# One fused model block on one Trainium2 core: wide bias reads, one load of x, one turn for two norms, last combine over eight banks, two value groups 512 columns wide

## The reference, cut to what matters

```python
# block 1, x is [512, 1024] f32
z = rms_norm(x, norm_mix) @ w_in                       # u | q k v of 8 heads of 64
y_pool = multiscale_pool(u, ...)
y_attn = neighbourhood_attention(q, k, v, rpb)         # 8x64 grid, window 8 rows x 16 columns, bias from rpb
x = x + concat(y_pool, y_attn) @ w_out
x = x + expert_choice_ffn(rms_norm(x), ...)            # 16 experts, 64 tokens each, 25 MB of weights each
x = x + sigmoid(rms_norm(x, norm_ple) @ w_ple_gate) * rms_norm(p @ w_ple_proj)
# block 2
x = gmlp_layer(x, c, ...)
shift, scale = ada_mod(c, kv_ada_w, ...)
k, v = split((rms_norm(x, kv_g) * (1 + scale) + shift) @ w_kv)     # 3 groups x 2 heads of 128, each
shift, scale, gate = ada_mod(c, b_ada_w, ...)
q, z = split((rms_norm(x, b_g) * (1 + scale) + shift) @ w_in_b)    # the same x: 3 groups x 8 heads of 128
o = three dilated attentions (dilations 1, 4, 16), merged by their log sums
x = x + gate * ((o * silu(z)) @ w_out_b)
```

## Time and profile before

| | |
|---|---|
| time, median of 3 runs | 2253.64 us (2252.07 to 2254.20) |
| profiled execution, its own time | 2254.82 us |
| its span, first to last instruction | 2252.8 us |
| TensorE busy | 2063.3 us (92%) |
| VectorE, ScalarE, GpSimd busy | 926.1, 565.2, 47.8 us |
| mean granted clock of TensorE | 0.949 |
| experts' weights | 3 x 128 slabs of 1 MB |

### The profile page before, as it was taken

One profiled execution on the slowest core, in us unless ns is written; L12 is line 12 of the kernel. 1 busy time (PEld: TensorE's weight loads), 2 busy tenths in 40 slices (PEclk: granted clock), 3 DMA queues, 4 the chain that ended last, 5 costly groups with the idle time before them and its releaser, 6 DMA issues.

```text
span 2252.8 us, 24571 instructions
## 1 busy us (share of the span) xinstructions
PE 2063.3 (92%) x9309; PEld 1235.3 (55%) x9309; DVE 926.1 (41%) x1483; ACT 565.2 (25%) x974; POOL 47.8 (2%) x53
## 2 busy tenths in 40 slices
PE   5999989999999999999999789999999998989798
PEld 4766763332222222222222277888887786867687
DVE  2776451111111111111111255465455727696963
ACT  3332341111011010111110244432232323553510
POOL 3050000000000000000000000000000000000000
PEclk9975799999999999999999898999999999989899
DMA  9641239999999999999999834454242212011010
GB/s 182 224 135 57 82 145 393 422 422 422 422 422 422 422 422 422 422 422 422 422 422 422 332 112 150 172 184 138 94 171 75 75 40 90 21 57 56 20 38 38
DMA packets 134346, 529.81 MB, mean 235 GB/s; under 512 B 10374, under 2 KB 58308, under 8 KB 85124
## 3 DMA queue, kind: packets, MB, share of 16 engines
q1 hardware_dynamic: 131988, 523.69, 59.5%
q0 software_dynamic: 1712, 3.06, 1.1%
q10 hardware_dynamic: 576, 2.10, 0.4%
HBM read 526.56 MB, written 2.23 MB: 235 GB/s over the span
## 4 chain that ended last, share of the span: by engine, by line
PE 54%; DMA 33%; DVE 7%; SPq 2%; ACT 2%; issue 1%; ACTq 0%; DVEq 0%
DMA w_expert<-in_w_up 15%; DMA w_expert<-in_w_gate 15%; PE bank L757 6%; PE bank L758 6%; PE bank L759 6%; PE bank L947 6%; PE bank L777 5%; PE bank L779 5%; PE bank L778 5%; DMA raw<-in_w_in 2%; PE bank L834 2%; PE bank L789 1%; PE bank L848 1%; PE bank L957 1%; SPq L616 1%
## 5 line engine op out<-in xcount | busy, mean ns | idle before, releaser
L947 PE MATMUL bank<-w_expert,chosen 128*64 128x512 f32 x2048 | 483.7, 602 | 62.4 <-DMA w_expert<-in_w_up 46.2
L947 PEld LDWEIGHTS bank<-w_expert,chosen 128*64 128x64 f32 x2048 | 130.4, 136 | 395.7 <-issue 232.6
L757 PE MATMUL bank<-act_hi,w_hi 128*128 128x512 f32 x656 | 271.0, 413 | 18.6 <-DVE w_lo L1423 14.7
L1423 DVE TENSOR_TENSOR w_lo<-raw,w_hi 128x2048 fp32r<-128x2048 f32 x75 | 171.9, 2292 | 219.8 <-ACT w_hi L1149 219.8
L758 PE MATMUL bank<-act_lo,w_hi 128*128 128x512 f32 x656 | 257.1, 392 | 0.0
L759 PE MATMUL bank<-act_hi,w_lo 128*128 128x512 f32 x656 | 256.9, 392 | 0.0
L1661 DVE TENSOR_TENSOR x_res<-x_res,bank 128x512 f32<-128x512 f32 x136 | 87.4, 684 | 412.2 <-PE bank L966 412.2
L957 PE MATMUL bank<-w_expert,hidden_t 128*64 128x512 f32 x1024 | 229.9, 596 | 6.0 <-ACT hidden_t L1295 4.6
L1149 ACT CAST w_hi<-raw 128x2048 fp32r<-128x2048 f32 x75 | 142.6, 1901 | 199.9 <-PE bank L779 165.7
L1683 DVE TENSOR_TENSOR hidden_rows<-gate_silu,bank 128x512 f32<-128x512 f32 x32 | 20.6, 684 | 364.4 <-PE bank L947 364.4
L757 PEld LDWEIGHTS bank<-act_hi,w_hi 128*128 128x128 f32 x656 | 124.0, 189 | 56.4 <-DVE w_lo L1423 16.5
(11 more groups left out here) (239 smaller groups left out, 2465.4 us busy)
## 6 DMA issues: line engine op xcount, KB each, us to landing
w_expert<-in_w_gate SPq DMA_DIRECT2D x128, 1024.0 KB, 24.9
w_expert<-in_w_up SPq DMA_DIRECT2D x128, 1024.0 KB, 26.5
w_expert<-in_w_down SPq DMA_DIRECT2D x128, 1024.0 KB, 26.2
raw<-in_a_w_in SPq DMA_DIRECT2D x24, 1024.0 KB, 5.7
raw<-in_b_w_in SPq DMA_DIRECT2D x16, 1024.0 KB, 5.3
raw<-in_a_ada_w SPq DMA_DIRECT2D x12, 1024.0 KB, 5.1
raw<-in_b_ada_w SPq DMA_DIRECT2D x12, 1024.0 KB, 6.0
raw<-in_w_in SPq DMA_DIRECT2D x8, 1024.0 KB, 10.7
```

Source lines behind the costliest of these rows:

```text
L757: mm(b[:, :], hi[:, cols], ah[:, kc, :], start=(kc == 0), stop=False)
L947: last = mm(PS[b0 + n][HALF[x], :], XE[:, k % 4, HALF[k // 4]], WE[place][:, r], start=(k == 0), stop=(k == KD - 1), skip_group_check=True)
L1423: tt(WLO[w % 2][:, :], RAW[slot(n_of["W"][w])][:, :], WHI[w % 2][:, :].bitcast(F32), ALU.subtract).then_inc(lo_ready, 1)
```

## The change

1. **Bias.** `rpb_wide` is flat with 16 floats behind it. `BIAS` holds 63 floats per row in place of 48 and is read by two DMAs of 64 partitions, each partition in one piece of 4032 floats (16,128 bytes). They wait until ScalarE has copied chunk 3 of the first projection. `V1` moves from 176.5 to 112 KB to make room.
2. **x.** ScalarE's queue loads x once, in plain order, and behind it slab 0. The transposes of `norm(0)` write to the bank in grid order (`grid_tile`, a stride of eight elements). SyncE's second load of x is gone; `c_wins` and the bias row of the gate are loaded behind slab 7 in place of slab 1. The transpose of the parameter rows stands between the first six chunks and the last two, so that the eighth chunk's bank is that of chunk 0.
3. **Last combine.** Eight matmul results go to eight banks with no wait in between. VectorE adds them first and norms behind them, with the lower part of the first gate slab before the last norm tile and that of the second behind `norm_lo`. ScalarE casts the first gate slab, does the statistics and `norm_hi`, then casts the second.
4. **One turn.** For keys and values `norm(4)` goes into `BH`, `BL`; ScalarE copies each bank to `XT` as well. The queries' norm is scaled from `XT` into `AH`, `AL`, four chunks ahead of the copies of the values of groups 1 and 2 and four behind them. TensorE has no `norm(5)`.
5. **Values.** Group 0 goes by two chunks of `fm_chunk` into `VF` (in the place of `GATE_A`) and is turned by eight transposes. Groups 1 and 2, whose token order is the same, share one unit: 128 tokens stationary (stride four), 512 columns moving, over two slabs.

```diff
-    rpb_wide = nc.dram_tensor("rpb_wide", (ROWS, H1 * ROWS, 63), F32, kind="Internal").ap()
+    rpb_wide = nc.dram_tensor("rpb_wide", (ROWS * H1 * ROWS * 63 + 16,), F32, kind="Internal").ap()
...
-        V1 = at("v1", 176.5, [P, NT, 512])
-        BIAS = at("bias_master", 184.5, [P, H1 * ROWS, 48])
...
+
+        BIAS = at("bias_master", 176.5, [P, H1 * ROWS, 63])
...
-        W_VK = [slab("W", fm_src(a["w_kv_2"], 768 + 256 * g)) for g in range(NG)]
+        W_V0 = slab("W", fm_src(a["w_kv_2"], 768))
+        W_V12 = tm_slabs(a["w_kv_2"], 0, 1, 1024)[0]
...
+            if k == 5:
+                count["lo"] += KD
+                return
...
+                if k == 0 and kc == 6:
+                    note(("cols",), "dve")
...
+        def grid_tile(b, t):
+
+            return b[:, :].rearrange("p (c r) -> p r c", r=ROWS)[:, 2 * t:2 * t + 2, :]
...
-            for n in range(N_E - 1):
+            for n in range(1, N_E - 1):
                 load(n)
-                if n == 3:
-                    sp.wait_ge(n_xn, NT)
-                    for t in range(NT):
-                        sp.dma_start(X[:, t, :], a["x"][0, t * P:(t + 1) * P, :]).then_inc(s_x, 16)
-                if n == 1:
+                if n == 7:
                     sp.dma_start(CW[:, :], c_wins).then_inc(s_wins, 16)
...
-            pool.wait_ge(s_rpb, 16 * (ROWS + 1))
-            for c in range(16):
-                pool.dma_start(BIAS[c * ROWS:(c + 1) * ROWS, :, :],
-                               bass.AP(rpb_wide.tensor, c, [[H1 * ROWS * 63, ROWS], [63, H1 * ROWS], [1, 48]])
+            pool.dma_start(rpb_wide[ROWS * H1 * ROWS * 63:].rearrange("(a b) -> a b", a=1), RPB[0:1, 0, 0:16]).then_inc(s_rpb, 16)
+            pool.wait_ge(s_rpb, 16 * (ROWS + 2))
+            pool.wait_ge(freed["act"], fills[("in", 3)][2])
+            for half in range(2):
+                pool.dma_start(BIAS[half * 64:(half + 1) * 64, :, :].rearrange("p k j -> p (k j)"),
+                               bass.AP(rpb_wide.tensor, 8 * half, [[1, 8], [H1 * ROWS * 63, ROWS], [1, H1 * ROWS * 63]])
                                ).then_inc(s_bias, 16)
...
             pool.dma_start(WP[:, :, :], a["w_pool"][0].rearrange("g c d -> c g d")).then_inc(s_wp, 16)
-            pool.wait_ge(freed["act"], fills[("in", 3)][2])
...
+                        pe.wait_ge(d_add, ADDS - 2 if chunks[0] == 0 else ADDS)
                     for t in range(NT):
...
-                            last = nc.tensor.transpose(banks[kc][:, t * P:(t + 1) * P],
+                            last = nc.tensor.transpose(grid_tile(banks[kc], t) if k == 0 else banks[kc][:, t * P:(t + 1) * P],
...
+                    if k == 0 and chunks[0] == 0:
+                        pe.wait_ge(s_rows, 16 * (len(COL_ROWS) + 2))
+                        b = begin(("cols",))
+                        nc.tensor.transpose(b[:, 0:NCOL], ROWS_IN[0:NCOL, :], ident[0:NCOL, 0:NCOL]).then_inc(filled, 1)
...
+            pe.wait_ge(v_xe, NE + 1)
             for t in range(NT):
-                combine(t, 8 * NE)
-            pe.wait_ge(v_xe, NE + 1)
+                for x in range(2):
+                    mm(PS[2 * t + x][:, :], SELT[HALF[x], t * P:(t + 1) * P], Y[HALF[x], :], start=True, stop=True
+                       ).then_inc(m_c, 1)
...
-                fm_chunk(W_K[j // 2], j % 2, ("k2", j), AH, AL, 50 if j == 0 else None)
+                fm_chunk(W_K[j // 2], j % 2, ("k2", j), BH, BL, 50 if j == 0 else None)
...
-            for g in range(NG):
-                hi, lo = slab_ready(W_VK[g])
+            for c in range(KV2):
+                fm_chunk(W_V0, c, ("vf", c), BH, BL)
+            banks = []
+            for s in range(2):
+                hi, lo = slab_ready(W_V12[s])
                 for t in range(NT):
-                    b = begin(("v2", g, t))
-                    for kc in range(KD):
-                        a_hi, a_lo = tile_of(AH[:, kc, :], g, t), tile_of(AL[:, kc, :], g, t)
-                        r = slice(kc * 256, (kc + 1) * 256)
-                        mm(b[:, 0:256], a_hi, hi[:, r], start=(kc == 0), stop=False)
-                        mm(b[:, 0:256], a_hi, lo[:, r], start=False, stop=False)
-                        last = mm(b[:, 0:256], a_lo, hi[:, r], start=False, stop=(kc == KD - 1))
-                    last.then_inc(filled, 1)
-            norm(5)
+                    if s == 0:
+                        banks.append(begin(("v12", t)))
+                    for k in range(4):
+                        kc = 4 * s + k
+                        a_hi, a_lo = tile_of(BH[:, kc, :], 1, t), tile_of(BL[:, kc, :], 1, t)
+                        r = slice(k * 512, (k + 1) * 512)
+                        mm(banks[t][:, :], a_hi, hi[:, r], start=(kc == 0), stop=False)
+                        mm(banks[t][:, :], a_hi, lo[:, r], start=False, stop=False)
+                        last = mm(banks[t][:, :], a_lo, hi[:, r], start=False, stop=(kc == KD - 1))
+                    if s == 1:
+                        last.then_inc(filled, 1)
+                if s == 0:
+                    last.then_inc(half_used, 1)
+            pe.wait_ge(freed["act"], fills[("vf", 1)][2])
+            for t in range(NT):
+                b = begin(("v0", t))
+                for c in range(KV2):
+                    last = nc.tensor.transpose(b[:, c * P:(c + 1) * P], VF[:, c, t * P:(t + 1) * P], ident)
+                last.then_inc(filled, 1)
...
             for t in range(NT):
-                grid = bass.AP(a["x"].tensor, a["x"].offset + t * P // ROWS * D, [[D, P // ROWS], [S // ROWS * D, ROWS], [1, D]])
-                act.dma_start(X[:, t, :], grid).then_inc(s_xg[t], 16)
+                act.dma_start(X[:, t, :], a["x"][0, t * P:(t + 1) * P, :]).then_inc(s_x[t], 16)
+            act.dma_start(raw3(0, KD), stream[0][0]).then_inc(loaded[0], 16)
             split_at, f = [0], [0]
...
 
+            split_upto(W_PGATE[0][0])
+            stats(2, lambda t: (d_add, 8 * NE + 2 * t + 2))
+            norm_hi(2)
             split_upto(W_PGATE[0][1])
-            stats(2, lambda t: (d_add, 8 * NE + 2 * t + 2))
             act.wait_ge(k_step, 25)
             nc.scalar.activation(ERSTD, ESS, ACT.Sqrt).then_inc(k_exp, 1)
-            norm_hi(2)
...
-            norm_full(4)
+            for kc in range(KD):
+                b = take(("norm", 4, kc))
+                scaled(b[:, :], NORM_MUL[4](kc), NORM_ADD[4](kc), kv_full)
+                nc.scalar.copy(XT[:, kc, :], b[:, :]).then_inc(freed["act"], 1)
...
-                for t in range(NT):
-                    nc.scalar.copy(V2[:, g, t, :], take(("v2", g, t))[:, 0:256]).then_inc(freed["act"], 1)
+            split_upto(W_V0 + 1)
+            for c in range(KV2):
+                nc.scalar.copy(VF[:, c, :], take(("vf", c))[:, :]).then_inc(freed["act"], 1)
+            split_upto(W_V12[1])
             act.wait_ge(freed["dve"], fills[("k2", 5)][2])
-            norm_full(5)
+            for kc in range(4):
+                scaled(XT[:, kc, :], NORM_MUL[5](kc), NORM_ADD[5](kc), b_full)
+            split_upto(W_V12[1] + 1)
+            for t in range(NT):
+                nc.scalar.copy(V2[:, 1:3, t, :], take(("v12", t))[:, :].rearrange("p (g d) -> p g d", g=2)
+                               ).then_inc(freed["act"], 1)
+            for kc in range(4, KD):
+                scaled(XT[:, kc, :], NORM_MUL[5](kc), NORM_ADD[5](kc), b_full)
+            for t in range(NT):
+                nc.scalar.copy(V2[:, 0, t, :], take(("v0", t))[:, 0:256]).then_inc(freed["act"], 1)
...
+                add_combined(j, 8 * NE, PS[j])
+                if j in (3, 5, 7):
+                    norm_tile(2, j // 2 - 1)
+            split_upto(W_PGATE[0][0])
+            norm_tile(2, NT - 1)
+            norm_lo(2)
             split_upto(W_PGATE[0][1])
-            for j in range(8):
-                add_combined(j, 8 * NE)
-                if j % 2 == 1:
-                    norm_behind(2, j // 2)
...
-            norm_split(4)
+            for kc in range(KD):
+                split_full(BH[:, kc, :], BL[:, kc, :], kv_full, kc + 1)
...
-            for g in range(1, NG):
-                split_upto(W_VK[g] + 1)
-            norm_split(5)
+            split_upto(W_V12[1])
+            for kc in range(KD):
+                split_full(AH[:, kc, :], AL[:, kc, :], b_full, kc + 1)
+                if kc == 3:
+                    split_upto(W_V12[1] + 1)
```

51 lines of the change are left out of this document (27 added, 24 removed).

## The result

| | before | after |
|---|---|---|
| time, median | 2253.92 us (2252.07 to 2254.53) | 2204.87 us (2198.66 to 2205.09) |
| span of the profiled execution | 2252.8 us | 2203.2 us |
| mean granted clock | 0.949 | 0.951 |

The ratio is 0.9777, with a 95% interval of 0.9759 to 0.9795: 49 us faster. The forecast was 2212, with a range of 2198 to 2226.

The account below looks back on a forecast made before the run. It took full DMA engines (422 GB/s) to bound the experts' loop and TensorE the rest. Terms 11.8 + 3.3 + 22.0 + 4.8 = 41.9 us off 2254.8 gave 2212.9, median 2212 us, range 2198 to 2226.

Parts of the forecast that it names:

- start: First projection, edits 1 and 2: 17.0 us of stall and low clock removed, less 2.0, 0.9 and 2.3; net 11.8 us.
- last combine: Tail of the experts, edit 3: last norm tile 6.2 us earlier, less 2.9 for low clock; net 3.3, bounds 1 and 6.2.
- values: Values, edit 5: 56.3 us before, 34.3 after with wide shared matmuls; 22.0 us gained.
- one turn: Queries and keys, edit 4: first query chunk 6.7 us shorter, keys' norm 1.9 us longer; net 4.8 us.
- the time of slab 0: Start: slab 0, queued behind x, is cast at 19.0 instead of 17.04, 2.0 us later; bounds 0 and 4.7.
- rival (b): First stall stays in part or whole, through x and slabs or slow new reads: 10 to 17 us lost, 2222 to 2229; chance 0.08.
- a gain ahead of the loop passes through whole: Experts' loop: nothing in it changes and its slab stream only starts earlier, so no earlier gain is lost.
- The lower bound: Values of groups 1 and 2: strided loads overlap running matmuls, 0.233 us each, 22.4 us; upper bound 32.9.
- rival (a): Values: strided loads do not hide behind 512-column matmuls; 10.8 us more, 2223; chance 0.12.
- The keys' norm: Keys, edit 4: ScalarE scales and also copies each bank, adding 1.9 us to the path.
- (c): First attention runs at the high clock, VectorE setting it at about 75 us: 35 us less, 2177; chance 0.05.
- (d): Experts' slab stream slows, for example to 395 GB/s: loop 65 us longer, 2277, slower than before; chance 0.03.

Follow-up runs that it names:

- warm_all: Kernel after, with extra identity transposes filling TensorE's idle time at the start, ahead of the experts' first gather and around the last combine's norm; 2196.0 us.
- narrow_early: Kernel after, with the bias read back in 16 DMAs of 192-byte pieces, issued without waiting for chunk 3; x still loaded once; 2213.3 us.
- x_twice: Kernel after, with x loaded in grid order first and again in plain order behind slab 3; slab 0 still behind x, bias reads wide; 2209.4 us.
- warm_folds: warm_all plus extra transposes around the dilated attentions and their merge, and throughout the first attention, including idle time under VectorE's folds; 2170.8 us.
- warm_first: warm_all plus 26 transposes before the first attention's first transposes and 4 in each later item; 2200.6 us, executions 2180.2 to 2215.3.

## Why the prediction was right, point by point

The time, 2204.9, lies 7 us below the 2212 of the forecast and inside the range. By its terms:

| term | forecast | traces | undone on the chip |
|---|---|---|---|
| start | 11.8 | 18.2 | bias 8.4 (9.9 at the border), x 4.6 (7.3) |
| given back ahead of the experts | none | -3.5 | 3.4 (warm_all) |
| last combine | 3.3 | 5.2 | 4.9 |
| values | 22.0 | 22.0 | 21.7 |
| one turn | 4.8 | 6.0 | 5.1 |
| merge | none | 1.6 | not tested |
| sum, profile | 41.9 | 49.6 | |

The misses cancel in part, and that is luck: the start, the last combine, the turn and the merge gained 11.1 more than forecast, and 3.5 that I had at nothing were given back. The merge has a clock of 0.52 before and 0.68 after in the ten microseconds where it starts; why is open.

**Start: right in mechanism, mis-sized by 6.4.** The step that failed is the time of slab 0: x landed at 13.5, 1 MB at half of 385 GB/s in 5.5 us, a cast at 19.0. It took x's time of arrival from before and so carried the slow grid-order load into a kernel that no longer has it. The prediction's "large pieces ran at 385 and more everywhere outside the stretch of the small ones" was a wrong reading of the same kind: x in pieces of 4 KB had moved at 224. It also priced the bias reads at 5 us; at 205 to 210 GB/s their 2.06 MB take 10, inside the bounds and hidden. x in plain order comes at about 360 GB/s, and the cast came 3.6 us earlier where I had it 2.0 later; the bounds (0 to 4.7 later) left out a gain. The rest held: the 14.7 us of idle time and the 2.3 behind it are gone, the last transposes stand ahead of the first matmul (seven take 1.76 us at the low clock, where I had 0.9 for eight), and that matmul starts at 19.78, 2.3 us earlier than before, with the low clock at its first matmuls costing 1.5 where I took 2.3. Together 2.3 + 14.7 + 2.3 - 1.5 = 17.8 of the 18.2.

How the 18.2 divide between the two edits hangs on their order. With the narrow reads kept, edit 2 takes the border of the start from 136.41 to 128.11 (narrow_early), 8.3 us; the wide reads then take it to 118.18, 9.9 more. I had given all 17.0 of the stall to the reads and a loss to edit 2. An early slab 0 put slab 3 ahead of the slow stretch, and TensorE's idle time there fell from 14.7 to 7.2 us with narrow reads in both. So rival (b), that x has a part in the stall, was right in that much. What the wide reads alone would gain, with edit 2 undone in full, was not run; x_twice does not show it.

**Ahead of the experts: a step that the prediction lacks.** That a gain ahead of the loop passes through whole was wrong by 3.5 us. The stream of slabs did start earlier, but the loop's first matmul waits for a gather on TensorE. That gather ran at 1.2 GHz behind idle time that had grown from 1.85 to 3.28 us, which cost 2.65 us; with that time filled it runs at 2.4 GHz again, and the stretch up to the experts' last slab gains 3.4. The other 0.8 us of the 3.5 were lost in and behind the first attention and are not explained.

**Last combine.** The last norm tile ends 1277.04 - 1263.15 = 13.9 us behind the cast of the gate's slab in place of 1299.13 - 1277.90 = 21.2, so 7.3 where I had 6.2. The low clock then took 2.1, forecast 2.9.

**Values and the turn.** The lower bound held, 0.235 us per matmul against 0.233, and rival (a) at 0.34 is out. The Trainium skill, "TensorE: Matmul & The Clock Gate", section Step-by-step: what each phase is for, has the load run beside the running matmul, and the trace agrees (a load of 310 ns in place of 188 cost 0.0085 us of pace); that the load's time goes by columns alone the trace contradicts again (310 ns strided, 188 not). The keys' norm cost 0.65 us where I had 1.9. The 1.9 do not follow from the prediction's own numbers (0.78 + 0.58 - 0.1 - 1.07 = 0.19 a pair, 1.5 in all), and the overlap was too small: each of the two starts before the one ahead of it ends, and the pair repeats every 1.14 us, 0.08 more than the 1.065 of before:

```profile
1727.58 0.84 ACT L1209 ACTIVATE full<-bank,stats 128x512 f32<-128x512 f32 x1
1728.26 0.64 ACT L1392 COPY x_turned<-bank 128x512 f32<-128x512 f32 x1
1728.72 0.86 ACT L1209 ACTIVATE full<-bank,stats 128x512 f32<-128x512 f32 x1
```

**Rivals (c) and (d)** did not come: clock and rate of the earlier trace rows are unchanged. But (c) was worth a test. At the full clock the stage takes 98.5 us from its first scores to the next split in place of 117; I had priced it at 35 us, by VectorE as the bound. With 296 extra transposes TensorE is all but never idle there, so whether fewer would do is open.

## What to carry to other kernels

When a load changes its access pattern, work out its arrival anew; a time read from the old trace belongs to the old pattern. Where an edit removes a wait of TensorE, look at the next place where it idles: when its own work ends sooner and the chain on another engine takes as long as ever, the gap grows, and the matmuls behind it may run at half clock. A low clock over a stage that looks busy need not be a property of the stage: look for idle time at its head and inside it, and try transposes into a bank that will be overwritten; here that was worth 34 us, where the whole change was worth 49. Fill all of it: with a part filled the executions spread over 35 us.

## What the runs showed that I had not expected

- Extra work made the kernel faster: with the idle gaps filled the mean clock is 0.994 and the time 2170.8, against 0.951 and 2204.9.
- The first attention, at 0.50 over 110 us with TensorE busy for 106 of them, did not find the full clock again by being busy; it kept it where 2.04 us of idle time under a fold were filled (warm_folds), and lost it where they were not (warm_first). Its one fall in warm_folds stands behind 16 matmuls of one column, with TensorE busy.
- Pieces of 16 KB to each partition, all from overlapping addresses one float apart, moved 205 to 210 GB/s at a share of 0.96 to 1.01, half of what the experts' slabs reach. The wide reads are hidden, not fast.
- The stretches in which x is loaded in grid order, in rows of 4 KB, moved 224 to 228 GB/s, in plain order 356 to 370 in the kernel after.
